# Output projection by token blocks, a second normalisation in two token halves, prefetched gates and two extra panel places in a hybrid encoder layer on one Trainium2 core

## The reference

```
h = rms_norm(x, norm_mix_w) * (1 + scale1) + shift1
u = h @ w_in                              # attention, HGRN2, RWKV-7 inputs and 3 x 1024 gate columns
o_a, o_b, o_c = diff_attention(...), hgrn2(...), rwkv7(...)
merged = sigmoid(g0) * (o_a @ w_a) + sigmoid(g1) * (o_b @ w_b) + sigmoid(g2) * (o_c @ w_c)
x1 = x + gate1 * (merged @ w_out)
h2 = rms_norm(x1, norm_ffn_w) * (1 + scale2) + shift2
a, b = split(h2 @ ffn_w_in)               # 2 x 2816 columns
x2 = x1 + gate2 * ((silu(a) * b) @ ffn_w_out)
out = rms_norm(x2, final_norm_w)
```

## Time and profile before

| | before |
|---|---|
| median of 3 runs | 1332.21 us (1330.75 to 1332.92) |
| the profiled execution, its own time | 1333.33 us |
| its span in the profile | 1331.5 us |
| PE busy | 1158.8 us (87%) |
| DVE busy | 667.0 us (50%) |
| ACT busy | 468.6 us (35%) |
| mean granted PE clock | 0.946 of full speed |

### The profile page before, as it was taken

The page is one execution under the profiler, slowest core; times in us unless marked ns, Lnnn a source line. Parts: engine busy times, 40 slices in busy tenths (PEclk is TensorE's granted clock), DMA queues, the critical chain, the costliest instruction groups (busy, mean ns, idle before and its releaser), DMA issues.

```text
span 1331.5 us, 17755 instructions
## 1 busy us (share of the span) xinstructions
PE 1158.8 (87%) x7421; PEld 936.4 (70%) x7421; DVE 667.0 (50%) x926; ACT 468.6 (35%) x546; POOL 28.0 (2%) x45
## 2 busy tenths in 40 slices
PE   2699999788999988788888889887899999999985
PEld 2588757567887676677656667665788888878864
DVE  4867564354343357883483553745544333333335
ACT  4322532122232535443523654513522222222222
POOL 0200000000000000000000000100000000000000
PEclk9999989889999999888978999889899999999988
DMA  7866423111013431004611114752243222222201
GB/s 265 275 218 216 133 78 116 57 49 42 11 42 119 151 127 40 32 32 142 213 64 56 42 54 135 240 185 96 100 138 127 95 95 95 95 95 95 95 0 63
DMA packets 105463, 143.93 MB, mean 108 GB/s; under 512 B 3028, under 2 KB 86088, under 8 KB 105384
## 3 DMA queue, kind: packets, MB, share of 16 engines
q1 hardware_dynamic: 91816, 105.76, 24.2%
q0 software_dynamic: 6080, 23.40, 5.0%
q10 hardware_dynamic: 7488, 13.63, 2.6%
HBM read 127.05 MB, written 15.73 MB: 107 GB/s over the span
## 4 chain that ended last, share of the span: by engine, by line
PE 66%; DVE 19%; ACT 11%; issue 2%; DMA 1%; ACTq 0%; DVEq 0%; SPq 0%; POOL 0%
PE bank L1784 65%; DVE wlo L1146 3%; ACT whi L759 3%; DVE ada_acc L1149 2%; DVE mg L1146 1%; DVE Z L1146 1%; DMA raw<-in_ada_w 1%; ACT Z L1006 1%; ACT Z L1004 1%; DVE qk L1146 1%; ACT gate_row L774 1%; DVE q_lev L1146 1%; ACT sg L1102 1%; DVE x L1146 1%; DVE k_lev L1146 1%
## 5 line engine op out<-in xcount | busy, mean ns | idle before, releaser
L1784 PE MATMUL bank<-hhi,whi 128*128 128x512 f32 x816 | 333.6, 409 | 13.1 <-DVE wlo L1146 10.3
L1146 DVE TENSOR_TENSOR wlo<-raw,whi 128x2048 fp32r<-128x2048 f32 (+1 forms) x82 | 175.4, 2139 | 328.8 <-ACT whi L759 328.1
L1784 PE MATMUL bank<-hlo,whi 128*128 128x512 f32 x816 | 324.2, 397 | 0.0
L1784 PE MATMUL bank<-hhi,wlo 128*128 128x512 f32 x816 | 323.7, 397 | 0.0
L759 ACT ACTIVATE whi<-raw 128x2048 fp32r<-128x2048 f32 (+1 forms) x82 | 146.8, 1790 | 222.4 <-PE bank L1784 205.0
L1784 PEld LDWEIGHTS bank<-hhi,whi 128*128 128x128 f32 x816 | 157.3, 193 | 56.6 <-DVE wlo L1146 11.4
L1784 PEld LDWEIGHTS bank<-hhi,wlo 128*128 128x128 f32 x816 | 157.0, 192 | 34.2
L1784 PEld LDWEIGHTS bank<-hlo,whi 128*128 128x128 f32 x816 | 157.6, 193 | 31.7 <-issue 0.5
L1784 PE MATMUL bank<-whi,d_hi 128*128 128x512 f32 x176 | 70.1, 398 | 7.7 <-DVE d_lo L1146 7.7
L1784 PE MATMUL bank<-wlo,d_hi 128*128 128x512 f32 x176 | 70.2, 399 | 0.0
L1784 PE MATMUL bank<-whi,d_lo 128*128 128x512 f32 x176 | 69.4, 394 | 0.0
(11 more groups left out here) (314 smaller groups left out, 1598.6 us busy)
## 6 DMA issues: line engine op xcount, KB each, us to landing
raw<-in_w_in SPq DMA_DIRECT2D x33, 1024.0 KB, 5.5
raw<-in_ada_w SPq DMA_DIRECT2D x24, 1024.0 KB, 5.3
raw<-in_f_in SPq DMA_DIRECT2D x22, 1024.0 KB, 5.0
early_out<-gate_row ACTq DMA_DIRECT2D x52, 256.0 KB, 2.0
raw<-in_f_out SPq DMA_DIRECT2D x11, 1024.0 KB, 4.8
sg<-early_out POOLq DMA_DIRECT2D x4, 1536.0 KB, 11.3
raw<-in_w_out SPq DMA_DIRECT2D x4, 1024.0 KB, 8.0
x_in<-in_x POOLq DMA_DIRECT2D x4, 512.0 KB, 7.8
```

The lines of the kernel that those rows point to most:

```text
L1146: return v.tensor_tensor(out_, a, b, op)
L1784: return t.matmul(out_, lhsT, rhs, start=start, stop=stop, skip_group_check=True)
```

## The change

- **Gates.** Two more places for gates and third-branch results, `sg2`, `br2` and `sg3`, `br3`, lie in the space of `hhi` and `hlo`, which is free between the last early product and the second normalisation. POOL starts all four reloads without waiting for merged blocks, and reloads `x` after the first merged block. ACT splits one branch panel more in front, and runs the sigmoid of block j+1 between the two splits of block j. DVE takes the panels in step.
- **Output projection.** PE waits for merged blocks one by one. The first half is as before; the second half runs token block by token block, with both panels `o(1,0)` and `o(1,1)` resident, the second of them in a new place, slot 2 (`spare_hi`, `spare_lo`).
- **Second normalisation.** Tokens 0 to 255 are normalised, transposed, scaled and split while `out(1,3)` and `f(0,0)` run, then tokens 256 to 511. The pieces are 128x256. `f(0,0)` runs as 96 matmuls of 256 columns in place of 48 of 512.
- **Panel calls around the FFN.** ACT splits up to `f(0,0)` before the normalisation, as before, but has no split at the head of block 0 of the FFN. DVE takes one panel at block 0 of the FFN, not two. The numbers of the panels that the later calls concern move accordingly.
- **FFN.** The four `ada` panels move from blocks 0 to 3 to blocks 3 to 6 (`FFN_LATE`). The last panel, d(10), goes to slot 3, in the space of `hhi` and `hlo`, and its split has to wait only for the last unit of FFN up.

```diff
+FFN_LATE = 3
...
-        if late:
+        if j >= FFN_LATE and late:
...
+def panel_slots():
+
+    spare = 2 * (FFN // 256) + FFN // 256 + 1
+    total = len(panel_ends())
+    slots = [2 if m == total - spare else 3 if m == total - 1 else (m + (m > total - spare)) % RING for m in range(total)]
+    freed_by = []
+    for m, slot in enumerate(slots):
+        earlier = [k for k in range(m) if slots[k] == slot]
+        freed_by.append(earlier[-1] if earlier else None)
+    return slots, freed_by
...
-        sg = [at("sg0", 0, [P, 3, 2, T]), at("sg1", 48, [P, 3, 2, T])]
-        br = [at(f"br{j}", (12, 72, 88, 12)[j], [P, 2, T]) for j in range(4)]
+        sg = [at("sg0", 0, [P, 3, 2, T])[:, :, :, :], at("sg1", 48, [P, 3, 2, T])[:, :, :, :]]
+        sg += [nc.alloc_sbuf_tensor_at(f"sg{2 + n}", [P, 3, 2, T], F32, offset=place)[:, :, :, :] for n, place in enumerate(h_place)]
...
+        spare_hi = at("spare_hi", 36, [P, 2048], F32R)
+        spare_lo = at("spare_lo", 44, [P, 2048], F32R)
...
+        last_hi, last_lo = (tile[:, 0:4, :].rearrange("p k t -> p (k t)") for tile in (hhi, hlo))
+        hi_slots = [whi[:, 0, :], whi[:, 1, :], spare_hi[:, :], last_hi]
+        lo_slots = [wlo[:, 0, :], wlo[:, 1, :], spare_lo[:, :], last_lo]
...
-            pool.wait_ge(*full("early", E_RW + 7))
-            for j in range(4):
-                if j == 1:
-                    pool.wait_ge(*full("da pt", 4 * TB - 1))
-                elif j >= 2:
-                    pool.wait_ge(s_mg_sum, 2 * j - 2)
-                reload(br[j][:, :, :], E_RW + 2 * j, 2, s_branch_in[j])
-                reload(sg[j % 2][:, :, :, :].rearrange("p g m t -> p (g m) t"), e_gates(j), 6, s_gates_in[j % 2])
+            for j, ready in enumerate((("early", E_RW + 7), ("da pt", 4 * TB - 1), ("early", N_EARLY - 1), None)):
+                if ready:
+                    pool.wait_ge(*full(*ready))
+                reload(br[j], E_RW + 2 * j, 2, s_branch_in[j])
+                reload(sg[j].rearrange("p g m t -> p (g m) t"), e_gates(j), 6, s_gates_in[j])
             gate_bias(1)
 
-            pool.wait_ge(s_mg_sum, 8)
+            pool.wait_ge(s_mg_sum, 2)
...
-                if m >= RING:
-                    slot_released(act, m - RING)
-                do(whi[:, m % RING, 0:src.shape[1]], src, ACT.Copy).then_inc(s_panel_hi, 1)
+                if freed_by[m] is not None:
+                    slot_released(act, freed_by[m])
+                elif m == len(weights) - 1:
+                    act.wait_ge(*full("ffn", FFN // 256 - 1, 1, 1))
+                do(hi_slots[slots[m]][:, 0:src.shape[1]], src, ACT.Copy).then_inc(s_panel_hi, 1)
...
-            act.wait_ge(s_da_lo, 4)
+
+            def gate(j):
+
+                act.wait_ge(s_gates_in[j], 16)
+                do(sg[j], sg[j], ACT.Sigmoid).then_inc(s_gated, 1)
+                act.wait_ge(s_gated, up(s_gated))
+
+            split_hi()
+            gate(0)
             for j in range(4):
                 split_hi()
+                if j < 3:
+                    gate(j + 1)
                 split_hi()
-                act.wait_ge(s_gates_in[j % 2], 16 * (j // 2 + 1))
-                do(sg[j % 2][:, :, :, :], sg[j % 2][:, :, :, :], ACT.Sigmoid).then_inc(s_gated, 1)
-                act.wait_ge(s_gated, up(s_gated))
                 for m in range(2):
                     act.wait_ge(s_mg_sum, 2 * j + m + 1)
                     do(mg_hi[:, 2 * j + m, :], mg[:, m, :], ACT.Copy).then_inc(s_mg_hi, 1)
                     act.wait_ge(s_mg_hi, up(s_mg_hi))
-            for n in range(4):
-                split_hi()
-            norm(1, x1, x1_norm)
+            split_hi()
+            split_hi()
+            split_hi()
+            norm(1, 0, x1, x1_norm)
+            norm(1, 1, x1, x1_norm)
+            for n in range(2 * KC):
+                if n == 4:
+                    norm(1, 2, x1, x1_norm)
+                elif n == 8:
+                    norm(1, 3, x1, x1_norm)
+                second_h(n)
 
             for j in range(FFN // 256):
                 for which in range(2):
-                    split_hi()
+                    if j or which:
+                        split_hi()
                     if which == 0:
                         for m in range(2):
...
-            for j in range(4):
-                take_panel()
-                take_panel()
-                gates, other = sg[j % 2], br[j]
+
+            def other(j):
+
                 dve.wait_ge(s_gated, j + 1)
                 dve.wait_ge(s_branch_in[j], 16)
-                tt(other[:, :, :], gates[:, 2, :, :], other[:, :, :], ALU.mult).then_inc(s_dve_step, 1)
+                tt(br[j], sg[j][:, 2, :, :], br[j], ALU.mult).then_inc(s_dve_step, 1)
                 dve.wait_ge(s_dve_step, up(s_dve_step))
+
+            take_panel()
+            other(0)
+            for j in range(4):
+                gates = sg[j]
                 for m in range(2):
...
+                take_panel()
+                if j < 3:
+                    other(j + 1)
...
-            for n in range(3):
                 take_panel()
+
+            norm_scale(1, 0, KC)
+            take_panel()
+            take_panel()
             dve.wait_ge(s_x_again, 16)
-            for n in range(2):
-                if n:
+
...
+            for tb in range(TB):
+                add_mix(0, tb)
+            take_panel()
+            for tb in range(2):
+                add_mix(1, tb)
+                row_rstd(1, tb)
+            add_mix(1, 2)
+            second_scaled(0)
+            for n in range(2 * KC):
+                if n == 3:
+                    row_rstd(1, 2)
+                elif n == 5:
+                    add_mix(1, 3)
+                elif n == 7:
+                    row_rstd(1, 3)
+                if n == KC - 1:
+                    second_low(n)
+                    second_scaled(n + 1)
+                else:
+                    second_scaled(n + 1)
+                    second_low(n)
+
+            for j in range(FFN // 256):
+                if j:
                     take_panel()
...
-                if j < 4:
-                    ada_out(20 + j)
+                if FFN_LATE <= j < FFN_LATE + 4:
+                    ada_out(20 + j - FFN_LATE)
...
-            pe.wait_ge(s_merged, KC)
-            for n in range(2):
-                moving_units((mg_hi, mg_lo), [("out", n, tb) for tb in range(TB)])
-            transposes(1, x1_norm, range(KC))
-
+            tiles = [begin("out", 0, tb) for tb in range(TB)]
+            for half in range(2):
+                slot = next_panel()
+                for tb, ps in enumerate(tiles):
+                    for k in range(4):
...
+            out_slots = [next_panel(), next_panel()]
+            for tb in range(TB):
+                if tb == 3:
+                    second_transposes(0, range(6))
+                ps = begin("out", 1, tb)
...
+                end(last, "out", 1, tb)
+            second_transposes(0, range(6, 8))
+
+            slot = next_panel()
+            first = [begin("ffn", 0, 0, m) for m in range(2)]
+
...
+            first_units(0, range(KC))
+            second_transposes(1, range(6))
+            first_units(1, range(2))
+            second_transposes(1, range(6, 8))
+            first_units(1, range(2, KC))
             for j in range(FFN // 256):
                 for which in range(2):
-                    slot = next_panel()
-                    for m in range(2):
-                        stationary_unit(slot, m, h_in, KC, "ffn", j, which, m, h_from=None if j or which or m else KC)
-                    if which == 0 and j < 4:
+                    if j or which:
+                        slot = next_panel()
+                        for m in range(2):
+                            stationary_unit(slot, m, h_in, KC, "ffn", j, which, m)
+                    if which == 0 and FFN_LATE <= j < FFN_LATE + 4:
                         late_ada()
```

216 lines of the change are left out of this document (134 added, 82 removed).

## The result

| | before | after |
|---|---|---|
| median | 1331.48 us (1327.67 to 1332.92, 4 runs) | 1434.34 us (1430.89 to 1435.61, 4 runs) |
| ratio, 95% interval | | 1.0773 (1.0743 to 1.0803) |
| the profiled execution, its own time | 1333.33 us | 1433.56 us |
| its span, mean granted clock | 1331.5 us, 0.946 | 1431.7 us, 0.930 |

What follows compares the result with a forecast made beforehand. PE was taken as the bound, busy 87% of the span. Front -28.4, FFN up idle +93.6, low clock +46.0 and FFN down -0.8 make +110.4 us on 1333.3, so 1443 us for the median, range 1422 to 1467.

Steps and rivals of the forecast that it cites:

- Branch stage: Branch products before the output projection: 192 matmuls and one late panel take 45.6 us instead of 57.0, gain 11.4.
- Output projection: After the branches: no stop ahead, gain 5.1 us; 192 matmuls without low clock in 44.6 against 47.75, gain 3.1.
- Normalisation: Second normalisation, before the transposes: PE's idle 12.1 us go, leaving some 0.3 us of waiting for `hlo` pieces.
- 256-column matmuls: `f(0,0)`: 96 matmuls at 0.171 us take 16.4; the stage with transposes and waits costs 21.4, a loss of 3.3.
- Front in all: From the first branch product to the end of `f(0,0)`: 28.4 us gained.
- The stops of FFN up: FFN up and entry of FFN down: late panel calls make PE stand idle at next panels, 93.6 us.
- The clock: Half clock behind FFN up's stops: 2.5 us after each of twelve, 1.6 after each of ten, 46.0 us.
- FFN down and the last panel: FFN down: nothing late in steady state; stop before the last block 5.4 us against 6.2, gain 0.8.
- The rival without clock loss: FFN up: PE keeps full clock through stops of this size, so the end is 1397 us; chance 0.06.
- The rival with longer low clock: FFN up: a loss of some 4.5 us per stop, 99 instead of 46, so 1496 us; chance 0.04.
- The rival of a front that brings nothing: Front: panels stay late and 256-column pieces run at 0.232, so its gain goes, about 1471 us; chance 0.04.
- The look-ahead rival: FFN up: ACT and DVE finish panels before PE asks, no stops, only the front counts, 1303 us; chance 0.03.

Runs made afterwards that it cites:

- the same two: The kernel before with `if j or which` added before ACT's split and `if j` before DVE's take, making both late: 1462.28 us.
- the kernel with both calls ahead: The changed kernel without `if j or which` before ACT's split and `if j` before DVE's take, so both run one panel ahead: 1300.37 us.
- the kernel with the take ahead and the split late: The changed kernel with only `if j` before DVE's take removed, ACT's split left late: 1383.97 us, one execution.
- with the take late: The changed kernel with only `if j or which` before ACT's split removed, DVE's takes left late: 1355.84 us, one execution.

## Why the prediction was right, and where it was off

The forecast of the sum was +110.4 us against the profiled execution; the traces differ by +100.2. By its own steps:

- **Branch stage: right.** 45.6 us predicted with one late panel, `b(1,1)`; 46.05 measured (813.67 to 859.72), and the one stop is `b(1,1)`'s, of 0.77 us. Undoing the gates' part alone brings its two old stops back.
- **Output projection: right.** 44.6 us predicted, 45.38 measured, at full clock and with no stop ahead. 12 of the 32 transposes, some 1.2 us, ran inside it, where my sum had all of them in the next stage.
- **Normalisation: right in the main.** The 12.1 us have gone. The waits for `hlo` pieces are 1.30 and 0.64 us where I gave them 0.3.
- **256-column matmuls: mis-sized, by a row read wrongly.** I took 0.171 us, from rows of 128-column products, between bounds of 0.116 and 0.232. PE in order of time in `f(0,0)` of the changed kernel:

```profile
918.52 0.28 PE L1881 MATMUL bank<-hlo,whi 128*128 128x256 f32 x1
918.64 0.28 PE L1881 MATMUL bank<-hhi,wlo 128*128 128x256 f32 x1
```

They start every 0.12 us, close to the lower bound. 96 of them are 11.5 us instead of 16.4. The 0.171 was no price at full clock. The 5.48 us of the earlier trace rows hold both levels, as windows inside them in the kernel before show:

```profile
584.93:587.70 2.77, 2.77 (x14) 2.77 (x14) 2.43 (x3) 1.30 (x1) 0.00 (x0) 0.50 0.02 6
588.11:589.11 1.00, 1.00 (x11) 1.00 (x10) 0.41 (x2) 0.97 (x2) 0.00 (x0) 1.00 0.00 0
```

  At 0.50 the products of 128 columns start 0.21 us apart, at 1.00 they start 0.11 us apart, and 0.171 is the mean. The 0.146 us per transpose is such a mean too (0.81 over its 2.63 us). With 0.11 the row would have pointed at the lower bound. The stage took 17.55 us, some 18.8 with the 12 transposes that had run before it, where I had 21.4. That is a loss of 0.7 against the 18.1 before, below the 1.3 that I had named as its lower bound; the range had room for it (-5). The page "TensorE: Matmul & The Clock Gate" of the Trainium skill, section "Back-to-back issue gap", gives a formula that makes 109 ns for 256 columns, an estimate, without the weight load: the trace shows 120 ns, so it was nearer than the row I chose. By it the piece would have been 96 x 0.062 = 6.0 us shorter, not the "some 4" of the prediction. Front in all: 31.0 us gained, 28.4 predicted; the 1.2 us that the first two stages took more hide a part of what the third took less.
- **The stops of FFN up: right.** The waits for `wlo` are 93.4 us in 23 times, and 0.77 us of that is `b(1,1)`. So the 21 stops inside FFN up and the one at the entry of FFN down make 92.6 us, where the prediction's terms are 95.5 when the entry's 4.8 us stand whole. The rest is that I put the end of PE's last matmul 0.1 to 0.2 us earlier than the profile does. The period is 34.0 us, as forecast (963.30 to 997.29). The experiments show the cause: two conditions, 134 us, in the changed kernel; the same two, 130 us, in the kernel before. One term in it was mis-sized: the prediction takes off 3.6 us, 0.9 for each `ada` product that now lies in a stop. In the kernel before the last matmul of `f(0,0)` starts at 953.46 us, and the next product behind the `ada` product here:

```profile
954.36 0.58 PE L1784 MATMUL bank<-hhi,whi 128*128 128x512 f32 x1
```

  That is 0.90 us from start to start, of which 0.23 are the spacing. So an `ada` product held PE up by 0.67 us, the four by 2.7, and the term is 0.9 us too large.
- **The clock: right in kind, mis-sized, and the largest miss.** "12 x 2.5 + 10 x 1.6 = 46.0" took a loss of 2.5 us behind each stop of over 4 us, from the 13 matmuls in 5.64 and 12 in 5.25 us of the earlier trace rows. Behind stops of 5.10 us the changed kernel runs 14 in 5.00 and 13 in 4.71 us. At full clock matmuls start 0.227 us apart (37 spacings from 967.43 to 975.82 us in its trace), so these would take 3.18 and 2.95: a loss of about 1.8. Behind the stops of 6.66 and 3.17 us 15 run in 5.00 us, a loss of 1.6. Over all 21 stops inside FFN up, the 31 matmuls behind a stop take 180.1 us from first start to last start, and 142.9 at full clock. So the loss is 37.2 us, 1.6 to 2.0 per stop, no longer behind 6.66 us than behind 3.17, where the prediction's terms for these 21 make 43.5. (Some 0.15 of each is the first matmul's slower start and not the clock: behind the 1.67 us stop at the entry of FFN down in the kernel with both calls ahead, at full clock, the same count gives 0.15.) The mean clock of a period is 0.90, above the 0.85 that I had named as a sign. The table shows it in the second stretch: +131.5 us measured against 93.6 + 46.0 less the 2.5 behind the entry, 137.1. The 5.6 us between them are the clock's 6.3 less the 0.9 of the `ada` products, to within 0.2.
- **FFN down and the last panel: right.** The stop before the last block is 5.19 us where 5.4 was predicted (6.05 before), and the own place brings nothing, which two runs confirm. The stretch changed by -0.3 us where my terms made +1.7 (2.5 of low clock behind the entry, -0.8): again the clock, since 15 matmuls in 5.00 us at 0.68 are a loss of 1.6 behind the stop at the entry and behind the last:

```profile
1288.12:1293.12 5.00, 5.00 (x15) 3.99 (x16) 3.46 (x3) 0.00 (x0) 0.00 (x0) 0.68 0.73 223
1393.93:1398.93 5.00, 5.00 (x15) 3.99 (x16) 0.38 (x1) 0.00 (x0) 0.00 (x0) 0.68 0.01 3
```

The misses are 2.6 us (front), 5.6 (FFN up) and 2.0 (FFN down), all on the same side, and make the 10.2 us. The mechanism, its place and its length are those of the prediction; what was off are two prices, of the low clock and of the 256-column matmul. The rival without clock loss (1397) falls with the 0.59 to 0.68 of the windows. The rival with longer low clock (1496) falls too, though the kernel with the take ahead and the split late had 5 us wholly at 0.50 behind some of its stops. The rival of a front that brings nothing (1471) falls with the 31.0 us. The look-ahead rival, 1303 us, describes the kernel with both calls ahead (1300.37), which is what this change would have been without its two conditions.

What the prediction missed was not in the sum at all: that the `ada` move is worth about 10 us and the last place 6.5 once the calls are ahead. It made no difference to the forecast, as both act only where the late calls do not cover them.

## What to carry to other kernels

Where engines run fixed queues, read a moved or skipped producer call by what stands ahead of it: a split or a take that is called behind a wait for the consumer's current work has lost its look-ahead, even if the data and the buffer have long been there. Such a stop costs the producers' own time (3.2 or 5.1 us here) and 1.6 to 2.0 us of low clock behind it. Before a row is used as a price, read the granted clock of its own window: a mean over both levels is the price of neither. And judge the parts of a change one at a time: here 31 us of gain were in it, two conditions cost 134, and a buffer worth 6.5 us was worth nothing until they were undone.

## What was not expected of the hardware

- A matmul of 128 columns is hardly cheaper here than one of 256: at full clock products of 128 columns start 0.11 us apart (11 in 1.00 us, above), split matmuls of 256 columns 0.12, and split matmuls of 512 columns 0.227. PEld is busy for the whole of the window with 128 columns, and also in `f(0,0)` (1.17 us of 1.17 between 917.81 and 918.98). That fits a weight load that sets the pace of the short ones, but no run separates it from another cost of each matmul.
- The low clock behind a stop varies at the same stop length. Behind 4.4 us in the branch stage 13 matmuls took 5.64 us at 0.50; behind 5.10 us in FFN up 14 ran in 5.00 at 0.63. With two stops in 34 us, as in the changed kernel, the loss was 1.6 to 2.0 us each time. With one stop per block and the take ahead, it was near 1.5 and near 2.5 us in turn. Stops of 1.67 us in these stages left the clock at 1.00. A stop of 2.86 us before `f(0,1)` did both: with both calls ahead PE ran 15 matmuls in the next 5 us at 0.66 (above), and with the take late, which there gives the same stop, 22 at 1.00. In that same kernel one of the stops of 3.17 us left no low clock either, while others of that length had 15 matmuls in 5.00 us. The windows behind the 2.86 us and behind that 3.17 us stop, with the take late:

```profile
922.70:927.70 5.00, 5.00 (x22) 4.11 (x23) 0.67 (x1) 1.98 (x2) 0.00 (x0) 1.00 0.64 210
...
963.96:968.96 5.00, 5.00 (x22) 4.16 (x23) 2.27 (x1) 0.00 (x0) 0.00 (x0) 1.00 0.80 257
```

  What decides between these cases stays open; no run varied it alone. A price for the clock behind a stop of some 3 us is good to 1.7 us either way.
